# One-layer streaming encoder on one core: x also handed over channels first, and the first block of modulation sums shared by three engines

## The reference, cut to what matters

```python
cond = silu(c)                                  # 1024 values
mod = cond @ w_ada + b_ada                      # 1024 -> 6 * 1024
sh1, sc1, gt1, sh2, sc2, gt2 = split(mod, 6)
h = x * rsqrt(mean(x * x, axis=-1) + 1e-6) * g_pre_mix * (1.0 + sc1) + sh1
zin = h @ w_in                                  # 1024 -> 3072, 24 chunks of 128
...                                             # conv group, HGRN2 group, w_out
x = x + gt1 * rms_norm(mix, g_post_mix)
...                                             # SwiGLU feed-forward
```

## Time and profile before

| | us |
|---|---|
| median of 3 runs | 1127.38 |
| lowest and highest run | 1126.68, 1128.68 |
| span of the profiled execution | 1124.7 |
| first matmul of the projection (L2004) starts | 28.74 |
| first matmul of chunk 2 (L2041) starts | 65.77 |
| PE busy | 1089.5 (97% of the span) |

### The profile page before, as it was taken

The page is one execution under the profiler, slowest core; times in us unless marked ns, Lnnn a source line. Parts: engine busy times, 40 slices in busy tenths (PEclk is TensorE's granted clock), DMA queues, the critical chain, the costliest instruction groups (busy, mean ns, idle before and its releaser), DMA issues.

```text
span 1124.7 us, 14554 instructions
## 1 busy us (share of the span) xinstructions
PE 1089.5 (97%) x5140; PEld 907.7 (81%) x5140; DVE 823.3 (73%) x1168; ACT 498.9 (44%) x815; POOL 751.2 (67%) x645
## 2 busy tenths in 40 slices
PE   2899999999999999999999999999999999999996
PEld 1688888888888888888888888888888888888885
DVE  5977997979998755678775767666666666666658
ACT  5665575574652834345333323333333333233334
POOL 4179666675773640427977777868686969696966
PEclk9999999999999999999999999999999999999999
DMA  9644332333311271202322222222221222222217
GB/s 330 198 143 136 99 111 74 115 94 95 94 38 38 70 249 75 93 26 80 92 68 65 76 66 71 71 63 71 62 77 58 74 68 66 70 63 74 66 48 297
DMA packets 104745, 107.49 MB, mean 96 GB/s; under 512 B 6525, under 2 KB 84578, under 8 KB 104674
## 3 DMA queue, kind: packets, MB, share of 16 engines
q1 hardware_dynamic: 103216, 102.26, 29.0%
q10 hardware_dynamic: 1458, 4.31, 1.0%
HBM read 98.16 MB, written 8.40 MB: 95 GB/s over the span
## 4 chain that ended last, share of the span: by engine, by line
PE 94%; DVE 2%; ACT 1%; SPq 1%; issue 1%; DMA 1%; DVEq 0%; ACTq 0%
PE pair L2235 34%; PE pair L2041 23%; PE pair L2255 17%; PE pair L2144 8%; PE pair L2077 2%; PE pair L2198 2%; PE pair L2278 2%; PE pair L2004 1%; DMA x<-in_x 1%; DVE acc L1403 1%; PE pair L2072 1%; PE pair L2091 1%; PE pair L1965 1%; SPq L541 1%; PE pair L2093 1%
## 5 line engine op out<-in xcount | busy, mean ns | idle before, releaser
L1826 DVE TENSOR_TENSOR yt<-yt,pair 128x512 f32<-128x512 f32 x264 | 176.2, 684 | 34.6 <-PE pair L2255 34.6
L1524 DVE SCALAR_TENSOR_TENSOR pair<-u,conv_w_col,pair 128x512 f32<-128x512 f32 x208 | 139.6, 750 | 1.9 <-ACT pair L1120 1.4
L844 POOL TENSOR_TENSOR raw_r<-raw,w_hi 128x512 fp32r<-128x512 f32 x68 | 96.3, 1417 | 65.1 <-ACT w_hi L1256 65.1
L756 POOL TENSOR_TENSOR acc<-acc,ada 128x256 f32<-128x256 f32 x112 | 92.1, 854 | 55.9 <-ACT ada L1057 54.6
L2255 PE MATMUL pair<-w_hi,op_hi 128*128 128x512 f32 x280 | 109.2, 390 | 0.0
L2255 PE MATMUL pair<-w_hi,op_lo 128*128 128x512 f32 x280 | 109.0, 389 | 0.0
L2255 PE MATMUL pair<-w_lo,op_hi 128*128 128x512 f32 x280 | 108.9, 389 | 0.0
L853 POOL TENSOR_TENSOR w_lo<-w_lo_f,w_hi 128x512 fp32r<-128x512 f32 x70 | 95.1, 1359 | 0.0
L2235 PE MATMUL pair<-t_lo,w_hi 128*128 128x512 f32 x240 | 93.7, 390 | 0.0
L2235 PE MATMUL pair<-t_hi,w_hi 128*128 128x512 f32 x240 | 93.4, 389 | 0.0
L744 POOL TENSOR_TENSOR w_lo<-raw,w_hi 128x256 fp32r<-128x256 f32 x84 | 66.9, 828 | 23.1 <-ACT w_hi L1013 22.9
(11 more groups left out here) (330 smaller groups left out, 2951.0 us busy)
## 6 DMA issues: line engine op xcount, KB each, us to landing
ada<-in_w_ada SPq DMA_DIRECT2D x48, 512.0 KB, 3.9
raw<-in_w_ffn_in SPq DMA_DIRECT2D x56, 256.0 KB, 3.0
raw<-in_w_in SPq DMA_DIRECT2D x24, 512.0 KB, 3.8
w_lo_f<-in_w_ffn_out SPq DMA_DIRECT2D x40, 256.0 KB, 3.1
w_hi_f<-in_w_ffn_out SPq DMA_DIRECT2D x30, 256.0 KB, 3.1
x<-in_x SPq DMA_DIRECT2D x8, 512.0 KB, 8.2
raw<-in_w_out SPq DMA_DIRECT2D x8, 512.0 KB, 3.4
x<-in_x SPq DMA_DIRECT2D x4, 1024.0 KB, 8.7
```

Of the source, the lines that this page charges most:

```text
L756: i_ = pool.tensor_tensor(acc[:, cols], acc[:, cols], ada[:, n % 2, cols], ALU.add)
L844: pool.tensor_tensor(place_part(at), place_full(at), place_part(GU_HIGH[m % 3]), ALU.subtract).then_inc(gu_low, 1)
L1524: i_ = dve.scalar_tensor_tensor(out=dst, in0=tap_of(j + 1, h), scalar=tap_weight(j + 1, t), in1=dst, op0=ALU.mult, op1=ALU.add)
L1826: i_ = dve.tensor_tensor(dst, dst, bank(4 + t), ALU.add)
```

## The change

The host hands x over a second time, transposed (`in_xt`, channels first), so that `x0` holds 8 channel tiles of 1024 tokens. What was done on token tiles is done in another way:

- ACT squares each channel tile into one of two buffers. PE adds the squares of the 8 tiles over the partitions with a full matrix of ones, in float32, into two banks (`square_sums`). ACT makes the inverse root from them by Ln and Exp (`root0`, the same value in all partitions).
- DVE multiplies a tile by `gs` and `root0` (`scale_x`), ACT adds `mod` and rounds to the high part (`first_high`, `whole_high`), and DVE makes the low part (`first_low`). There are no transposes of x, and except for tile 0 each step covers all 1024 tokens. PE projects a tile with 12 matmuls.
- w_ada's shift and scale come in five blocks, `BLOCKS = [[0], [1], [2, 3], [4, 5], [6, 7]]`, without a ring. Block 0 is summed by DVE as before. For blocks 1 to 4 ACT multiplies rows 0 to 4 (`row_products`), POOL adds these five rows up with four additions (`add_rows`), and DVE multiplies and adds rows 5 to 7 (`sum_block`).
- POOL splits chunks 0 and 1 in quarters between its additions, and makes `masks_late` after the whole of `h` is ready, where it was made ahead of that wait.

The core of the diff:

```diff
+BLOCKS = [[0], [1], [2, 3], [4, 5], [6, 7]]
+ROWS_ACT = 5
...
             load_block(0)
-            for i in range(TT):
-                if i == 4:
-                    for g in range(RAW):
-                        load_chunk(g)
-                sp.dma_start(x0[:, i, :], x_d[:, i, :]).then_inc(x_loaded[i], 16)
-            for b in range(1, 4):
+            for i in range(KT):
+                sp.dma_start(x0[:, i, :], xt_d[:, i, :]).then_inc(x_loaded[i], 16)
+            for g in range(RAW):
+                load_chunk(g)
+            for b in range(1, len(BLOCKS)):
                 load_block(b)
...
+            def add_rows(b):
+                made = ROWS_ACT * (b - 1)
+                for n, (to, by) in enumerate(((0, 1), (2, 3), (0, 4), (0, 2))):
+                    pool.wait_ge(ada0_product, made + max(to, by) + 1)
+                    if n > 1:
+                        pool.wait_ge(ada0_added, rows_added(b - 1) + n)
+                    pool.tensor_tensor(ada_row(b, to), ada_row(b, to), ada_row(b, by), ALU.add).then_inc(ada0_added, 1)
+            for b in range(1, len(BLOCKS)):
+                for g in range(2):
+                    split_quarter(g, b - 1)
+                add_rows(b)
+            pool.wait_ge(acc_ready, len(BLOCKS))
             split_at(2)
+            pool.wait_ge(h0_ready, H0)
             mask_late()
-            pool.wait_ge(h_ready, 16)
...
+            for kt in range(KT):
+                act.wait_ge(x_loaded[kt], 16)
+                if kt >= 2:
+                    act.wait_ge(ss_summed, kt - 1)
+                act.activation(squared[kt % 2], x0[:, kt, :], ACT.Square).then_inc(sq_ready, 1)
+            act.wait_ge(ss_summed, KT)
+            for cols in HALF_COLUMNS:
+                me.done(act.activation(pair[2][:, cols], pair[2][:, cols], ACT.Ln, scale=1.0 / D, bias=EPS))
...
+            def row_products(b):
+                for j in range(ROWS_ACT):
+                    act.wait_ge(ada0_loaded[2 * b + j // 4], 32)
+                    act.activation(ada_row(b, j), ada_row(b, j), ACT.Copy, scale=cond[:, j:j + 1]
+                                   ).then_inc(ada0_product, 1)
...
+            row_products(1)
+            act.preload_act_table_set("sigmoid_and_others")
+            row_products(2)
+            whole_high(1)
+            whole_high(2)
+            row_products(3)
+            whole_high(3)
+            whole_high(4)
+            row_products(4)
+            for kt in range(5, KT):
+                whole_high(kt)
...
+            def sum_block(b):
+                dve.wait_ge(ada0_loaded[2 * b + 1], 32)
+                dve.wait_ge(ada0_added, rows_added(b))
+                for j in range(ROWS_ACT, KT):
...
+            sum_block(2)
             scale_shift(2)
+            scale_x(2)
             scale_shift(3)
+            scale_x(3)
+            first_low(2)
+            sum_block(3)
+            first_low(3)
             scale_shift(4)
+            scale_x(4)
             scale_shift(5)
+            scale_x(5)
+            first_low(4)
+            sum_block(4)
+            first_low(5)
             scale_shift(6)
+            scale_x(6)
             scale_shift(7)
+            scale_x(7)
+            first_low(6)
+            first_low(7)
...
+            for kt in range(1, KT):
+                if kt == 3:
+                    mod_sums(4)
+                    mod_sums(5)
+                if kt == 5:
+                    mod_sums(6)
+                    mod_sums(7)
+                pe.wait_ge(h0_ready, h0_count(kt, 1))
+                project_group(kt, (0, 1))
```

More of the change, by code:

```diff
@@ L73 @@
 OUT_HIGH = 5
-ADA_RING = 3
-GROUPS = [(0, 0), (1, 0), (0, 1), (1, 1)] + [(kt, half) for kt in range(2, KT) for half in range(2)]
+BLOCKS = [[0], [1], [2, 3], [4, 5], [6, 7]]
+BLOCK_OF = [b for b, kts in enumerate(BLOCKS) for _ in kts]
+ROWS_ACT = 5
+H0 = KT + 1
 M_SLOT = 5
@@ new lines, in _ @@
+            act.wait_ge(ss_summed, KT)
+            for cols in HALF_COLUMNS:
+                me.done(act.activation(pair[2][:, cols], pair[2][:, cols], ACT.Ln, scale=1.0 / D, bias=EPS))
+            for n, cols in enumerate(HALF_COLUMNS):
+                me.wait(behind=1 - n)
+                act.activation(root0[:, cols], pair[2][:, cols], ACT.Exp, scale=-0.5).then_inc(root_ready, 1)
+            def row_products(b):
[3 more added lines that the diff above has]
+                                   ).then_inc(ada0_product, 1)
@@ new lines, in first_high, with whole_high @@
+            def first_high(kt, cols, scaled):
+                act.wait_ge(x0_scaled, scaled)
+                act.activation(high_of(kt)[:, cols], x0[:, kt, cols], ACT.Identity, bias=mod[:, kt:kt + 1]
+                               ).then_inc(h0_hi, 1)
+            def whole_high(kt):
+                first_high(kt, slice(0, S), kt + 2)
+            act.wait_ge(vec_ready, 2)
+            act.activation(lb_tmp[:, 1, :], lb_tmp[:, 0, :], ACT.Exp).then_inc(cond_ready, 1)
+            for half, cols in enumerate(HALF_COLUMNS):
+                first_high(0, cols, half + 1)
@@ L1449, in _ @@
-            low_half(3)
-            sum_rows(1, range(4, KT))
-            sum_rows(2, range(2))
+            other_vectors()
+            for half, cols in enumerate(HALF_COLUMNS):
+                dve.wait_ge(root_ready, half + 1)
+                scale_x(0, cols)
+            for half, cols in enumerate(HALF_COLUMNS):
+                first_low(0, cols, half + 1)
+            sum_block(1)
+            scale_shift(1)
+            scale_x(1)
+            first_low(1)
+            sum_block(2)
@@ L2007, in project_group @@
+                    for s_, (a, x) in enumerate([(w_hi, high_of(kt)), (w_hi, low_of(kt)), (w_lo, high_of(kt))]):
+                        for half in halves:
+                            cols = HALF_COLUMNS[half]
+                            i_ = pe.matmul(pair[n][:, cols], a[:, n, w], x[:, cols], start=kt == 0 and s_ == 0,
+                                           stop=kt == KT - 1 and s_ == 2)
+                    if kt == KT - 1:
                         i_.then_inc(w_used, 1)
+            for kt in range(4):
+                square_sums(kt)
@@ L2008, in _ @@
             mod_sums(0)
-            mod_sums(1)
-            turn_x(0)
-            turn_x(1)
+            for kt in range(4, 6):
+                square_sums(kt)
             pe.wait_ge(vec_loaded, 16 * VEC_LOADS)
```

256 lines of the change are left out of this document (111 added, 145 removed).

## The result

The change made the kernel slower, and by more than forecast: 1150.62 us against 1127.95 us (medians of four runs each, taken together), a ratio of 1.020 (95% interval 1.019 to 1.022). The forecast was 1142.9, with 1149.8 as the upper end of the range. The span went from 1124.7 to 1148.2, 23.5 us more. Nearly all of it lies ahead of chunk 2, as the prediction said it would: the timeline of TensorE (start, us it took, engine, line, tiles) shows these rows, where before the first matmul came at 28.74 and chunk 2 at 65.77.

A forecast was written before the change was run, and what follows sets the result against it. TensorE bounds the kernel, through the start of chunk 2: head, two turns of the block chain and the tail put it at 81.3 instead of 65.77, 15.5 us later, so 1142.9 us from a median of 1127.38; range 1136.5 to 1149.8.

The forecast's parts named there:

- What bounds the kernel: TensorE, busy 97% of 1124.7 us; moving chunk 2's start (65.77) moves the kernel's end equally, unless VectorE or GpSimd are late.
- `sg` wait: Chunk 2's 0.61 us wait for ScalarE's `sg` goes, since chunk 0 is ready 1.36 us before chunk 1.
- chain through ScalarE's queue: Middle of first stage: products of blocks 3 and 4 queue behind high parts of tiles 2 and 4, so blocks run singly.
- its signs: ScalarE idle before high parts of tiles 2 and 4, GpSimd 2 to 5 us before additions of blocks 3 and 4.
- Head: Start to first matmul: first square 9.3, squares summed 25.9, first matmul 30.1, which is 1.4 us later than before.
- Turn 2 to 3: From GpSimd's first addition of block 2 to that of block 3: 12.85 us, from 36.0 to 48.85.
- four additions 5.35: GpSimd's four additions of a block within one turn, at 1.30 us per 512-column addition: 5.35 us.
- Turn 3 to 4: First addition of block 3 to that of block 4: 13.35 us, to 62.2, with `first_low(3)` 1.3 replacing the column sums.
- Tail: Behind block 4's first addition: additions, three rows, `first_low`, `scale_shift` and `scale_x` until 75.9; then tiles 6 and 7 until 81.3.
- TensorE's clock: After waits, tiles 1 to 5 begin at 1.2 GHz; tile 5 adds 0.8 us; slow tiles 6 and 7 would add 5.4.
- POOL is dearer: Rival: at 1.83 us each, the twelve additions of blocks 2 to 4 cost 6.4 more, giving 1149.3 us; 8%.
- DVE late start counts: Rival: VectorE's work behind the stage starts 3.9 us late, behind GpSimd's masks, and this costs time: 1146.8 us; 7%.

The follow-up runs named there:

- act_order: Kernel after the change, with ScalarE's products of blocks 3 and 4 moved right behind the high part of tile 1: 1147.4 us, ratio 1.017.
- short_dve: Kernel after the change, with VectorE's multiplication and low part of tile 1 cut to 8 of 1024 columns: 1148.0 us, ratio 1.017.
- no_additions: Kernel after the change, with GpSimd's sixteen additions left out, so rows 1 to 4 of blocks 1 to 4 are missing: 1135.4 us, ratio 1.007.
- split_late: Kernel after the change, with GpSimd's split of chunk 2 moved behind the wait for all of h: 1149.0 us, ratio 1.019.
- three_edits: Kernel after the change, with float32r squares and ones, ScalarE's products of blocks 3 and 4 early, and chunk 2's split behind all of h: 1136.6 us, ratio 1.007.
- dve_rows: Kernel after the change, with VectorE summing all eight rows of every block, no ScalarE products and no GpSimd additions: 1143.3 us, ratio 1.014.

## Why the prediction was right and wrong

The step that failed is the price of the work in the chain: the prediction took each engine's operations at the length that they have alone. For VectorE and GpSimd working at the same time it put nothing into the sum, and into the range only dearer additions on GpSimd (1.43 and 1.83 us). The steps and their order were right.

- **What bounds the kernel** was right: the start of chunk 2 carried the change, and behind it nothing moved by more than 1 us. The `sg` wait went as said. The chain through ScalarE's queue was right too, and its signs are there: ScalarE idle for 9.40 us ahead of the high part of tile 2, GpSimd for 4.62 and 5.09 ahead of the additions of blocks 3 and 4, VectorE for 5.34 and 5.67 ahead of their sums.
- **Head**: first square ready at 10.2 (9.3 forecast; the table was loaded 0.4 us later, and ScalarE waited 0.57 us for x), squares summed at 27.0 (25.9), first matmul 31.03 (30.1). A tile's sum cost 1.72 (1.74), so the price was right. With longer additions of block 1 (3.3 for 2.9) and quarters (2.6 for 2.2) the additions of block 2 began at 37.58 instead of 36.0: **1.6 us** of the 7.2 that chunk 2 is late against the forecast of 81.3.
- **Turn 2 to 3** is the step that failed most: 15.4 us instead of 12.85, **2.5 us**. The mechanism was right (the chain through ScalarE's queue, shown by `act_order`), the term "four additions 5.35" was too small: 7.37, since `scale_x(1)` and `first_low(1)` lie beside them. The prediction took 1.30 for an addition because "DVE is idle during most of the new additions"; at this block it was not. The three rows on VectorE took 2.7 beside GpSimd's quarters instead of 2.3, and VectorE got the column sums after 1.1 us instead of 0.8, with TensorE at 1.2 GHz. `short_dve` and `no_additions` show the first two apart: 5.29 for the additions, and 2.3 for the three rows.
- **Turn 3 to 4**: 13.95 for 13.35, **0.6 us**, the three rows again and `first_low(3)` at 1.74.
- **Tail**: 15.9 us from the additions of block 4 to the end of `first_low(6)`, for 13.7: **2.2 us**. The two `scale_x` cost 4.8 instead of 2.6. The prediction said of the split of chunk 2 only that it is in time, and gave it no price; `split_late` shows that it cost VectorE 2.3 us; there the same way takes 13.7 us, as forecast.
- **TensorE's clock**: tile 5 went at 1.2 GHz, as the range allowed, and tiles 6 and 7 at full speed (5.66 for 5.45): **0.2 us**. It was more than that once VectorE was quicker (`split_late`).
- **"POOL is dearer"** was the rival nearest to the result (1149.3), but with the wrong mechanism: the additions were 1.3 each when alone (two in 2.63 in block 4), and dear only beside VectorE (block 2), and more was lost on VectorE's side, which the rival left out. So that it came near is luck. "DVE late start counts" is contradicted: VectorE began 2.6 us after chunk 2 in after and 6.2 us after it in `three_edits` (83.15 against 76.98), and the rest of the span was 1059.7 and 1057.5.
- **The upper end of the range** took the dearer additions and left out that the two engines slow each other. Of the 7.2 us some 5.5 are this one cause (2.0 in the additions of block 2, 0.8 in the three rows of blocks 2 and 3, 0.4 in `first_low(3)`, 2.2 in the last two `scale_x`), which is why small terms had the same sign.

In this kernel the rows show that a VectorE instruction with two inputs in SBUF and a GpSimd instruction that reads SBUF hardly run side by side: `scale_x(7)` is done 1.08 us after the subtraction that was under way ended, and the subtraction itself had waited for `scale_x(6)` (3.23 for 2.39). The Trainium skill, SBUF — State Buffer, section Who interferes with whom, says this outright: a VectorE instruction with two SBUF inputs contends with a GpSimd instruction that reads SBUF. The Trainium skill, SBUF — State Buffer, section SBUF: two separate sides, adds that whichever of the two starts first has the shared pair of ports for its whole instruction while the other blocks. By that rule, the trace agrees (7.37 against 5.29, 3.08 against 1.28). The prediction had weighed the cycle count of the Trainium skill, GPSIMD Engine Reference, section 3.1 Elementwise, by which it estimated 1.1 us for an addition. The 1.31 measured for one alone is longer, as the 1.30 of the earlier trace rows had said.

## What to carry to other kernels

Sharing a small sum among three engines made each hand-over part of a chain, and VectorE alone (`dve_rows`) was quicker than the three. Before work is given to GpSimd, list what VectorE does at the same time with two inputs in SBUF and add up to the length of the one to the other for each overlap; it costs both sides. And price a plain float32 matmul by its entries in a trace (two here, for 512 columns and for one alike), and keep TensorE off long runs of one-column matmuls, within which its clock fell to 1.2 GHz here.

## What the runs showed of the hardware that was not expected

- VectorE and GpSimd block each other in both directions: a multiplication of 1024 columns 1.28 alone and 1.74 to 3.08 beside GpSimd, GpSimd's cast 1.04 and 1.89, its subtraction 2.39 and 3.23, four additions 5.29 and 7.37 to 7.93. The profile counts the wait as busy time, so no idle time shows it; only the length of equal rows does.
- TensorE that is busy without a gap can stay at the lower of its two clocks: 96 entries of one-column matmuls took 17.74 us, at a granted clock of 0.50 from 45 to 55 us.
- The granted clock can differ between executions at one and the same place: behind a wait of 0.7 to 1.1 us for `pmat` it fell in 8 of 16 traces, and the rest of the kernel was some 1.5 us longer in these.
- Sums by a full matrix of ones, four entries and 1.72 us for 1024 columns in plain float32, were two entries and some 1.2 us in float32r, which is short enough to follow the loads: the Ln behind the last tile's sum came 6 us sooner.
